# Second mixer of a two-block transformer kernel: when attention sinks are added, in what order turns and fills stand, stick breaking two pairs at a time, an earlier final scaling, and half-row score products

## What is computed

```python
# sliding window attention, 8 heads, with a sink logit per head
logits = einsum('bcqhgd,bckhd->bhgcqk', qc, kw) * HEAD_DIM ** -0.5 - slopes * dist
probs = softmax(concatenate([logits, sink], -1), -1)[..., :-1]
out   = einsum('bhgcqk,bckhd->bcqhgd', probs, vw)
# stick breaking attention, 8 heads
z = einsum('bqhd,bkhd->bhqk', q_blk, k) * dh ** -0.5
log_beta, log_keep = log_sigmoid(z), where(before, log_sigmoid(-z), 0.0)
suffix  = cumsum(log_keep, reverse=True) - log_keep
weights = where(before, exp(log_beta + suffix), 0.0)
out     = einsum('bhqk,bkhd->bqhd', weights, v)
```

## Time and profile before

| | us |
|---|---|
| median of 3 runs | 1940.37 (1939.26 to 1940.82) |
| profiled execution, its own time | 1935.49 |
| span from its first to its last instruction | 1933.7 |
| MLA pipeline, from its first scores to its projection | 259.3 to 298.7 |
| NSA pipeline | 775.9 to 838.3 |
| opening of the second mixer up to `vb` | 1044.6 to 1071.3 |
| `vb` and first scores | 1071.3 to 1087.5 |
| fills, sliding window and stick breaking up to values of pair 2 | 1087.5 to 1202.7 |
| gating, output projection | 1202.7 to 1257.1 |
| expert rows | about 1268 to the end |

### The profile page before, as it was taken

The page is one execution under the profiler, slowest core; times in us unless marked ns, Lnnn a source line. Parts: engine busy times, 40 slices in busy tenths (PEclk is TensorE's granted clock), DMA queues, the critical chain, the costliest instruction groups (busy, mean ns, idle before and its releaser), DMA issues.

```text
span 1933.7 us, 29225 instructions
## 1 busy us (share of the span) xinstructions
PE 1771.7 (92%) x11218; PEld 1413.9 (73%) x11218; DVE 1293.5 (67%) x2402; ACT 919.1 (48%) x1905; POOL 324.4 (17%) x336
## 2 busy tenths in 40 slices
PE   8999999999999999999999988989987787777777
PEld 8999989999999999699998778976432232222222
DVE  5565887556765576976656757886776766766454
ACT  5444555444544453764445436633544344344433
POOL 2000004000000000030000000523433333333331
PEclk9999999999999999999999989999999999999999
DMA  7555425965555545035555423679999999999998
GB/s 289 189 180 188 144 91 149 259 250 183 168 194 195 184 145 189 33 111 198 183 195 165 131 88 110 205 296 379 407 420 422 422 421 422 422 421 420 421 422 321
DMA packets 96139, 485.02 MB, mean 251 GB/s; under 512 B 10577, under 2 KB 10833, under 8 KB 62977
## 3 DMA queue, kind: packets, MB, share of 16 engines
q0 software_dynamic: 38544, 275.25, 37.0%
q1 hardware_dynamic: 57456, 207.90, 32.1%
HBM read 478.65 MB, written 4.46 MB: 250 GB/s over the span
## 4 chain that ended last, share of the span: by engine, by line
PE 58%; DMA 15%; DVE 9%; issue 9%; POOL 5%; ACT 3%; another core or an unknown queue 0%; POOLq 0%; SPq 0%; ACTq 0%; DVEq 0%
PE PS L549 16%; PE PS L550 16%; PE PS L551 16%; DMA raw<-uv,A 4%; PE PS L2212 3%; DMA XF<-uv,A 2%; DMA YL<-uv,A 2%; DMA YH<-uv,A 2%; PE PS L2233 2%; DVE WL L1040 2%; DMA raw<-wst 2%; POOL raw L659 1%; DMA XH<-uv,A 1%; DMA WH<-uv,A 1%; DMA WL<-uv,A 1%
## 5 line engine op out<-in xcount | busy, mean ns | idle before, releaser
L1040 DVE TENSOR_TENSOR WL<-raw,WH 128x1024 fp32r<-128x1024 f32 (+1 forms) x375 | 449.7, 1241 | 88.7 <-ACT WH L676 88.1
L549 PE MATMUL PS<-XH,WH 128*128 128x256 f32 x1616 | 461.1, 285 | 15.2 <-DVE WL L1040 6.5
L550 PE MATMUL PS<-XL,WH 128*128 128x256 f32 x1616 | 456.3, 282 | 0.0
L551 PE MATMUL PS<-XH,WL 128*128 128x256 f32 x1616 | 455.9, 282 | 0.0
L676 ACT ACTIVATE WH<-raw 128x1024 fp32r<-128x1024 f32 (+1 forms) x375 | 370.9, 1041 | 39.0 <-PE PS L551 16.7
L549 PEld LDWEIGHTS PS<-XH,WH 128*128 128x128 f32 x1616 | 306.5, 190 | 19.7 <-DVE A L1431 7.4
L550 PEld LDWEIGHTS PS<-XL,WH 128*128 128x128 f32 x1616 | 306.6, 190 | 0.2
L551 PEld LDWEIGHTS PS<-XH,WL 128*128 128x128 f32 x1616 | 306.4, 190 | 0.0
L983 ACT ACTIVATE A<-A,RTK 128x1 f32<-128x1 f32 x256 | 75.1, 293 | 298.1 <-DVE A L1640 294.9
L726 ACT ACTIVATE A<-A 128x256 f32<-128x256 f32 x88 | 36.8, 418 | 342.2 <-DVE A L1075 342.2
L549 PE MATMUL PS<-GH,WH 128*128 128x256 f32 x704 | 198.2, 282 | 1.1 <-DVE WL L1040 1.1
(11 more groups left out here) (318 smaller groups left out, 2989.3 us busy)
## 6 DMA issues: line engine op xcount, KB each, us to landing
raw<-wst SPq DMA_DIRECT2D x381, 512.0 KB, 4.6
raw<-wst SPq DMA_DIRECT2D x8, 384.0 KB, 3.5
vscr<-A POOLq DMA_DIRECT2D x1, 3072.0 KB, 37.5
A<-vscr POOLq DMA_DIRECT2D x1, 2048.0 KB, 22.4
C<-cst SPq DMA_DIRECT2D x1, 1236.5 KB, 10.5
raw<-uv,A POOLq DMA_INDIRECT x65
hT<-xin SPq DMA_DIRECT2D x2, 512.0 KB, 4.7
A<-vscr POOLq DMA_DIRECT2D x1, 1024.0 KB, 12.5
```

The costliest lines, as they stand in the source:

```text
L549: pe.matmul(o, wh, xh, start=start, stop=False, skip_group_check=True)
L550: pe.matmul(o, wh, xl, start=False, stop=False, skip_group_check=True)
L551: return pe.matmul(o, wl, xh, start=False, stop=stop, skip_group_check=True)
L1040: dv.tensor_tensor(WL[:, m % SPL, 0:w], raw[:, i % RAW, 0:w], f32(WH[:, m % SPL, 0:w]), ALU.subtract).then_inc(s_lo, 1)
```

## The change

1. In the sliding window, DVE's round is split into `scores(i)` (bias, maxima, the four small sink instructions, ending when ACT may start) and `normalise(i-1)` (sum with the sink's exponential, reciprocal, scaling). The wait for ACT's exponentials of pair i thus moves from round i to round i+1, behind scores(i+1), and pair i is scaled one round earlier than before (in round i+1, no longer in round i+2).
2. On PE, `turn(i-2)` stands ahead of fill i, no longer behind it; on ACT, the copy of the turned pair stands ahead of the output copy and of `hi` of fill i.
3. Stick breaking starts inside the rounds (logits of pairs 0 and 1 in round 5, softplus in round 6), and every step of it takes two pairs together. The rounds become 12, one for each fill. ACT does two exps and then two lns. `ZP` moves to another part of the same buffer.
4. The final scaling of `hT` (eight instructions of DVE) moves from fill 5 to a place behind `lo("va", 0)`, in the `vb` stage.
5. `hi` of `qa` 2 and 3 moves ahead of ACT's eight squares, and DVE's `lo` of `qa` 2 goes ahead of the four sums of squares, of `qa` 3 behind them.
6. MLA and NSA scores contract over the 64 (for the rotary part 32) rows of their own head alone, blk outside and e inside, so that neighbouring products use different rows of the array. The clearing of `KN`, `KP`, `KSW` and the waits for it are gone; the rotary columns of the heads are stored in another order.

```diff
-    rope = [... for h in range(4 * t, 4 * t + 4)]) for t in range(4)]
+    rope = [... for h in (4 * t, 4 * t + 2, 4 * t + 1, 4 * t + 3)]) for t in range(4)]
...
-            po.memset(KN[0], 0.0)
-            po.memset(KN[1], 0.0)
-            po.memset(KP, 0.0).then_inc(s_pad, 1)
...
+                if p == 6:
+                    lo("qa", 2, 0)
                 pairs(p)
+                if p == 6:
+                    lo("qa", 3, 0)
...
             lo("va", 0)
+            for kc in range(8):
+                ins = dv.scalar_tensor_tensor(out=hT[:, kc, :], in0=hT[:, kc, :], scalar=c("gains", 48 + kc, 49 + kc),
+                                              in1=RT[:, 0, :], op0=ALU.mult, op1=ALU.mult)
+            ins.then_inc(s_hf, 1)
             dv.wait_ge(s_qrs, 1)
             own(dv.reciprocal(RS, RS))
...
+            def normalise(j):
...
                 dv.wait_ge(s_ex, J_SWA + j + 1)
                 dv.wait_ge(s_snke, j + 1)
-                sink_sums[j] = own(dv.tensor_tensor(rs, rs, tmp, ALU.add))
+                own(dv.tensor_tensor(rs, rs, tmp, ALU.add))
+                own.wait()
+                own(dv.reciprocal(rc, rs))
...
+            for i in range(7):
+                rest = fill()
+                if i < 4:
+                    scores(i)
+                if 1 <= i < 5:
+                    normalise(i - 1)
+                if i >= 3:
+                    low_out(YL, YH, i - 3, 6, O_SWA + i - 3)
+                if i == 5:
+                    logits(0)
+                    logits(1)
+                if i == 6:
+                    softplus(0)
+                    softplus(1)
+                rest()
...
-                for e in range(2):
-                    for blk in range(2):
-                        ins = pe.matmul(PS[:, b0 + e, 128 * blk:128 + 256 * blk], Q[:, j, 128 * blk:128 * blk + 128],
-                                        KSW[e][:, 2 * m + j // 4, 0:128 + 128 * blk], start=True, stop=True, skip_group_check=True)
+                for blk in range(2):
+                    for e in range(2):
+                        r = slice(64 * e, 64 * e + 64)
+                        ins = pe.matmul(PS[:, b0 + e, 128 * blk:128 + 256 * blk], Q[r, j, 128 * blk:128 * blk + 128],
+                                        KSW[e][r, 2 * m + j // 4, 0:128 + 128 * blk], start=True, stop=True, skip_group_check=True)
...
+                if 0 <= i - 2 < 4:
...
+                    turn(J_SWA, i - 2, AST)
+                if i == 5:
+                    sb_logits(0)
+                    sb_logits(1)
+                fill()
+
+
+            sb_suffix(0)
+            sb_suffix(1)
             fill()
+            sb_logits(2)
+            sb_logits(3)
+            sb_values(0)
+            sb_values(1)
             fill()
             fill()
             sb_suffix(2)
+            sb_suffix(3)
             fill()
+            fill()
             sb_values(2)
```

More of the change, by code:

```diff
@@ L889, in swa_out, with log1p @@
                 copy_out(YH, j, 6, O_SWA + j)
+            def log1p(p):
+                for q in (p, p + 1):
+                    e1 = E1P[:, q % 2]
+                    ac.wait_ge(s_e1, q + 1)
+                    own(ac.activation(e1, e1, ACT.Exp))
+                own.wait()
+                for q in (p, p + 1):
+                    e1 = E1P[:, q % 2]
+                    ac.activation(e1, e1, ACT.Ln, bias=c("eps", 2, 3)).then_inc(s_e1l, 1)
             n = 4
             for i in range(n + 3):
-                if i >= 3:
-                    swa_out(i - 3)
-                fill()
                 if 0 <= i - 2 < n:
@@ L915, in act_program @@
                     ac.activation(tmp, tmp, ACT.Exp).then_inc(s_snke, 1)
-            def log1p(p):
-                e1 = E1P[:, p % 2]
-                ac.wait_ge(s_e1, p + 1)
-                own(ac.activation(e1, e1, ACT.Exp))
-                own.wait()
-                ac.activation(e1, e1, ACT.Ln, bias=c("eps", 2, 3)).then_inc(s_e1l, 1)
             def stick(p):
@@ L1114, in low_out, with attention @@
                 dv.tensor_tensor(dst[:, j, :], PS[:, o, 0:T], f32(hi_[:, j, :]), ALU.subtract).then_inc(s_ol, 1)
-            def attention(J0, n, ST_, bias, factor, low, sink=None, fill=None):
+            def attention(J0, n, ST_, bias, factor, low):
                 for i in range(n + 3):
-                    filled = fill() if fill else None
                     if 0 <= i - 2 < n:
@@ L1122, in attention @@
                         dv.wait_ge(s_ex, J0 + k + 1)
-                        if sink:
-                            own.wait(sink_sums[k])
                         rc = stats[:, 2, q]
@@ L1460, in sink @@
                 dv.tensor_tensor(tmp, sk, nm, ALU.add).then_inc(s_snk, 1)
+            def normalise(j):
+                q = j % 3
+                st = AST[:, q, :].rearrange("p (e k) -> p e k", e=2)
+                rs, rc = stats[:, 1, q], stats[:, 2, q]
+                tmp = small[:, 48 + 4 * q:52 + 4 * q].rearrange("p (e b) -> p e b", e=2)
                 dv.wait_ge(s_ex, J_SWA + j + 1)
                 dv.wait_ge(s_snke, j + 1)
-                sink_sums[j] = own(dv.tensor_tensor(rs, rs, tmp, ALU.add))
-            attention(J_SWA, 4, AST, swa_bias, None, lambda j: low_out(YL, YH, j, 6, O_SWA + j), sink, fill)
+                own(dv.tensor_tensor(rs, rs, tmp, ALU.add))
+                own.wait()
+                own(dv.reciprocal(rc, rs))
+                own.wait()
+                for e in range(2):
+                    for b in range(2):
+                        sl = st[:, e, 128 * b:128 + 256 * b]
+                        ins = dv.tensor_scalar(sl, sl, rc[:, e, b:b + 1], None, ALU.mult)
+                ins.then_inc(s_pn, 1)
             mk = c("sbmask").unsqueeze(1).broadcast_to([128, 2, 128])
@@ L1524, in dve_program @@
             rest = fill()
-            log_weight(2)
+            softplus(2)
             softplus(3)
             rest()
+            rest = fill()
+            log_weight(2)
+            log_weight(3)
+            rest()
+            rest = fill()
             weight(2)
-            log_weight(3)
+            weight(3)
+            rest()
+            lo("upab", 0)
             sb_low(2)
-            weight(3)
-            lo("upab", 0)
             sb_low(3)
```

144 lines of the change are left out of this document (62 added, 82 removed).

## The result

The changed kernel takes 1923.2 us (median of 4, 1920.3 to 1925.7) where the kernel before takes 1940.2 on the same chip: ratio 0.9916, 95% interval 0.9901 to 0.993. The forecast was 1926, the range 1917 to 1933. The profiled execution is one of 1920.3 us with a span of 1918.5, 15.2 us under that of before; the walk had 14.6. TensorE has as many instructions as before.

What follows compares the result with a forecast made beforehand. PE is busy 92% of the span, so time can only come from places where PE waits or another engine paces it. 5.0 + 0.6 + 0 + 9 = 14.6 us off 1940.4 gives 1925.8, so 1926; range 1917 to 1933.

Steps and rivals of the forecast that it cites:

- the walk: Step-by-step timing of the new order through the engines, summing to 14.6 us off the span of 1933.7.
- MLA, 5.0 forecast: MLA half-row scores: PE's round falls from 4.2 to 3.2 us, DVE then paces at 3.5; gain 5.0, from 0 to 6.
- 1.2 us less if the 32-row products overlap as well: MLA's eight products per pair, 2.7 us: 1.2 us less with full overlap, bounds 0 and 1.35, 1.0 taken.
- at 0.2 the gain would be about 2.5 us smaller: MLA: changing between 64 and 32 rows may drain TensorE; at 0.2 us per change the gain shrinks by about 2.5.
- the prediction's own sign of being wrong, rounds above 3.7: MLA: the prediction is wrong if rounds stay above 3.7 us.
- NSA, 0.6 forecast: NSA half-row scores: DVE stays full, so only the first bias, waiting 0.78 us for scores, comes earlier; gain 0.6 us.
- rival (e): NSA: clock falls to its lower level, 16 slow rounds cost 32 us, total 1958; 0.05 for slower, 0.02 for a tie.
- Opening and scaling, 0 forecast: Opening starts `vb` 4.6 us earlier, the moved scaling makes `vb` 3 wait 3.5 us; together 0, from -1.5 to +2.
- The rounds, 9 forecast: Second mixer's rounds: waits of 13.5 us for 18 and fewer slow stretches; gain 9 us, bounds 3 and 14.
- 1.8 us for each wait above 3.4 us, none for those near 2: Rounds: slow-clock cost counted behind each PE wait, 1.8 us above 3.4 us and none near 2.
- Rival (b): Rounds give back: engine chain longer than walked, each 2 us wait slows the clock; loop 3, MLA 4, total 1932; chance 0.15.
- the scaling would have been free in the 6.67 us of idle time: `vb` stage: 3.25 us of scaling would fit DVE's idle time before `lo` of `vb` 2, but the order puts it after.

Runs made afterwards that it cites:

- two groups for a pair: Changed kernel with MLA's products of a pair sorted by rows, all four of 64 then all four of 32, output wrong: 1914.8 us, ratio 0.9922 to before.
- the opening alone: Kernel before with only the opening's edits for qa 2 and 3, hT scaling left in its old place: 1925.5 us, ratio 0.9972.
- the second: Profile of the changed kernel run again with no edit: 1914.9 us, ratio 0.9914 to before, rounds 107.43 us.
- gap and three groups: Changed kernel with hT scaling ahead of the low part of va and MLA's pair products in three row-size groups: 1909.9 us, ratio 0.9895 to before.

## Why the prediction was right

**MLA, 5.0 forecast, 4.0 measured.** The mechanism held, the size of the pair's gain was off: 0.6 us and not 1.0. DVE's timeline in the changed kernel, to set beside the earlier trace rows:

```profile
261.55 1.02 DVE L1241 SCALAR_TENSOR_TENSOR A<-PS,C 128x384 f32<-128x384 f32 x2 [1.42 <-PE PS L1883]
...
272.35 0.17 DVE L1125 RECIPROCAL small<-small 128x4 f32<-128x4 f32 x1
...
279.45 0.42 DVE L1116 TENSOR_TENSOR XL<-PS,XH 128x256 fp32r<-128x256 f32 x1 [0.19 <-ACT XH L733]
...
286.94 0.17 DVE L1125 RECIPROCAL small<-small 128x4 f32<-128x4 f32 x1
```

The first bias comes 0.56 us earlier (forecast 1.0), and DVE still waits 0.19 us in the round shown, with TensorE busy 34.5 of MLA's 35.3 us: TensorE at 3.7 us a round stays the pace, where I had DVE at 3.5 and TensorE idle in each round. The step that failed is "1.2 us less if the 32-row products overlap as well": they do overlap, but each change between 64 and 32 rows costs 0.2. The text had this as a condition, "at 0.2 the gain would be about 2.5 us smaller"; it was 1.0 smaller. The forecast's pair of 1.7 us is what two groups take, and the kernel has four, so 0.4 us a pair was missing and not 0.6. Up to round 4 the gain was 2.5 us (forecast 2.8), in rounds 4 to 7 it was 1.6 (2.2). The rounds are on average (286.94 - 272.35) / 4 = 3.65 us on DVE, and 3.72 from one pair to the next on TensorE, so the prediction's own sign of being wrong, rounds above 3.7, was just reached. The Trainium skill (TensorEngine Tiling (Array Packing), Tiling Modes) says that changing the tiling mode drains TensorE. The three orders agree with it, at 0.20 us for each group of one row size.

**NSA, 0.6 forecast, 0.5 measured.** From NSA's first products to its end the lead grows from 4.44 to 4.98 us, and all of it is there at DVE's first bias (772.46 for 777.44), as forecast. DVE stayed full behind it, busy 37.8 of 39.0 us from 777 to 816. The clock stayed at 1.00 in this profile, so rival (e) didn't come; three of the experiments had two slow stretches at its start and one had one, and even there the time from the first scores to the last pair's was at most 0.7 us longer (45.3 for 44.6). With two stretches (two groups for a pair, 776.5 to 784.5 us), TensorE was busy 6.9 of 8.0 us where it had been busy 5.8, and DVE 7.8 for 7.7, so TensorE's slack took up most of them.

**Opening and scaling, 0 forecast, 0.07 measured.** `vb` came 4.8 us earlier (4.6), and `vb` 3 waited 3.43 us (3.5) with one slow stretch. Both halves are shown apart: the opening alone gains 4.8 us up to the first sliding window scores, and the scaling moved into DVE's idle time gives 4.7 back.

**The rounds, 9 forecast, 11.2 in the profile, 8.6 in the second.** The walk, shifted by the 5.0 us of lead, against the profile: fill 1 1089.0 and 1089.1, fill 3 1107.9 and 1108.4, fill 5 1129.6 and 1129.8, fill 6 1137.4 and 1137.3, fill 7 1152.0 and 1149.8, start of the values of pair 2 1188.4 and 1186.5. The waits: turns 2.0 and 2.1 (measured 1.9 and 2.0), fill 6 1.2 (0.7), the suffixes 3.4 and 1.0 (3.0 and 1.1); only values(1) was well off, 3.65 (2.5). In all that is 13.4 us forecast and 11.2 measured, for 18 before. The step that failed is "1.8 us for each wait above 3.4 us, none for those near 2": the size holds (1.7), the condition doesn't. The first profile has a stretch behind the second turn's wait of 2.0 us and one behind values(1)'s of 2.5, none behind the suffix's 3.0; the second has two there. The same kernel has 2 or 4 in its rounds, and 3 in both kernels that differ from it in MLA alone. That is 3.4 us, more than any step of the walk was off. Rival (b) thus was half there: slow stretches do come behind waits near 2 us at times. Of the 11.2 us of the first profile, 3.4 are two slow stretches fewer than before; the second has as many as before, and 8.6 us.

**What the prediction passed over.** It walked through the new order as a whole and never asked what each part of it is worth: no gain is shown for the turn's move by itself, nor for the pairing. And it saw that the scaling would have been free in the 6.67 us of idle time; that remark was worth 4.7 us at the first fill.

**The sum.** 4.0 for MLA, 0.4 between it and NSA, 0.5 for NSA, 0.1 and 11.2, less 1.0 behind the rounds, is 15.2. That it stands so near the walk's 14.6 is in part luck: MLA was 1.0 us too high and the rounds 2.2 too low, and the walk had nothing for the 0.4 and the 1.0, whose causes were not traced. The medians are 17.0 apart, within the interval of the ratio (13.6 to 19.2 us). (A slip in the chances: rival (e) has 0.05 for slower, the closing line 0.04.)

## What to carry to other kernels

On an engine that works in order, extra work fits into an idle time only if it stands in front of the instruction that waits, not behind it: 3.25 us of scaling cost 4.7 on one side of a low part and nothing on the other, and softplus steps put ahead of late low parts gave 4.3. When a wait is removed, look for its twin: in these rounds the wait moved between fill 6 and the suffix, and between turn and values, with the sum nearly the same (11.0 to 11.2 us), until VectorE's softplus stood ahead of what it had no need of. And take the clock's slow stretches off both sides before an edit of a few us is judged by one profile.

## What was not expected of the hardware

Half-row products of different row sizes cost 0.20 us per group of one size (2.11, 1.91 and 1.71 us for the same eight products in four, three and two groups), so they are to be sorted by row size where the sums allow.

The slow stretches come in equal portions of 1.7 us, one or two at a time. They also come where TensorE doesn't wait: in six of the experiments there are one or two between 746 and 756 us, in a stage in which TensorE is busy all but 0.4 us of 130 (here in the kernel with gap and three groups; the clock is the 0.99 and, in the ten us in which the stretch begins, the 0.89):

```profile
640.00:770.00 130.00, 129.62 (x1041) 126.90 (x1040) 85.52 (x129) 58.01 (x81) 1.81 (x4) 0.99 0.50 168
740.00:750.00 10.00, 10.00 (x81) 10.00 (x80) 5.12 (x8) 1.32 (x2) 0.00 (x0) 0.89 0.49 169
```

What decides between the executions stays open; none of the runs varied it alone.
